# Norms passed in two halves of the tokens, with the output projection and the MLP in one block

## What is computed

```python
h = rmsnorm(x, norm_mix_pre)
q, k, v, gate, u = split(h @ w_in)            # mixer 1: retention, and an S5 scan over u with a GLU
mix = concatenate([y_ret, y_ssm]) @ w_out
x = x + rmsnorm(mix, norm_mix_post)
h = rmsnorm(x, norm_mlp_pre)
m = square(relu(h @ w_ff1)) @ w_ff2           # 1024 -> 4096 -> 1024
x = x + rmsnorm(m, norm_mlp_post)
hx = rmsnorm(x, pre_mix_g) * (1 + sc1) + sh1  # block 2: mixer with a two-way scan and a pool mixer
mix_x = mixer(hx)                             # ends in a projection by w_out_2
x = x + g1 * rmsnorm(mix_x, post_mix_g)
hm = rmsnorm(x, pre_mlp_g) * (1 + sc2) + sh2
x = x + g2 * rmsnorm(square(relu(hm @ w_mlp1_2)) @ w_mlp2_2, post_mlp_g)
```

## Time and profile before

| | us |
|---|---|
| median of 3 runs (lowest, highest) | 3440.88 (3438.74, 3441.52) |
| the profiled execution's own time | 3440.63 |
| its span, first to last instruction | 3438.8 |
| PE matmuls busy | 2934.4 (85%) |
| DVE busy | 1477.4 (43%) |
| POOL busy | 794.1 (23%) |
| ACT busy | 564.4 (16%) |

### The profile page before, as it was taken

The page is one execution under the profiler, slowest core; times in us unless marked ns, Lnnn a source line. Parts: engine busy times, 40 slices in busy tenths (PEclk is TensorE's granted clock), DMA queues, the critical chain, the costliest instruction groups (busy, mean ns, idle before and its releaser), DMA issues. The chain is left out here.

```text
span 3438.8 us, 35085 instructions
## 1 busy us (share of the span) xinstructions
PE 2934.4 (85%) x13838; PEld 2435.9 (71%) x13838; DVE 1477.4 (43%) x1676; ACT 564.4 (16%) x672; POOL 794.1 (23%) x417
## 2 busy tenths in 40 slices
PE   3987976978999999996987988847488799999996
PEld 3766765777888888875775767646367688888885
DVE  6365362243222222235655578856734422222224
ACT  3212213121110000012221112111111100000001
POOL 1110111212333333330211211102122233333331
PEclk9977988979999999995998998868787899999998
DMA  3121113101222122121000321231120111111111
GB/s 113 49 62 45 47 58 131 42 25 62 67 70 64 61 68 67 61 67 70 30 26 31 110 74 55 73 117 67 61 80 25 31 44 48 49 49 43 49 49 55
DMA packets 60736, 205.61 MB, mean 60 GB/s; under 512 B 10160, under 2 KB 13488, under 8 KB 60400
## 3 DMA queue, kind: packets, MB, share of 16 engines
q1 hardware_dynamic: 39072, 140.16, 12.4%
q10 hardware_dynamic: 21584, 64.40, 5.5%
HBM read 173.99 MB, written 29.36 MB: 59 GB/s over the span
## 5 line engine op out<-in xcount | busy, mean ns | idle before, releaser
L185 POOL CAST w_hi<-w_raw 128x1024 fp32r<-128x1024 f32 x206 | 221.6, 1076 | 2571.3 <-PE ps L198 2536.3
L194 PE MATMUL ps<-a_hi,w_hi 128*128 128x512 f32 x2176 | 707.8, 402 | 94.1 <-PEq L2170 21.6
L196 PE MATMUL ps<-a_lo,w_hi 128*128 128x512 f32 x2176 | 693.6, 395 | 0.0
L198 PE MATMUL ps<-a_hi,w_lo 128*128 128x512 f32 x2176 | 692.1, 394 | 0.0
L187 POOL TENSOR_TENSOR w_lo<-w_raw,w_hi 128x1024 fp32r<-128x1024 f32 x206 | 572.3, 2778 | 16.5
L194 PEld LDWEIGHTS ps<-a_hi,w_hi 128*128 128x128 f32 x2176 | 414.2, 193 | 182.2 <-issue 100.3
L196 PEld LDWEIGHTS ps<-a_lo,w_hi 128*128 128x128 f32 x2176 | 416.8, 192 | 88.9
L198 PEld LDWEIGHTS ps<-a_hi,w_lo 128*128 128x128 f32 x2176 | 415.5, 191 | 88.8
L194 PE MATMUL ps<-g_hi_b,w_hi 128*128 128x512 f32 x1120 | 352.2, 396 | 92.6 <-DVE g_lo_b L2121 56.1
L198 PE MATMUL ps<-g_hi_b,w_lo 128*128 128x512 f32 x1120 | 349.2, 393 | 0.0
L196 PE MATMUL ps<-g_lo_b,w_hi 128*128 128x512 f32 x1120 | 349.1, 393 | 0.0
(11 more groups left out here) (379 smaller groups left out, 2675.1 us busy)
## 6 DMA issues: line engine op xcount, KB each, us to landing
w_raw<-in_wstream SPq DMA_DIRECT2D x206, 512.0 KB, 3.5
ada_w<-in_ada_w ACTq DMA_DIRECT2D x50, 512.0 KB, 3.5
y_by_token<-y ACTq DMA_DIRECT2D x16, 512.0 KB, 2.7
tmp_b<-mixer_out SPq DMA_DIRECT2D x8, 512.0 KB, 3.3
x_res_b<-in_xT SPq DMA_DIRECT2D x1, 4096.0 KB, 13.8
x_block<-x_res_b SPq DMA_DIRECT2D x8, 512.0 KB, 2.6
u_rows<-ada_w ACTq DMA_DIRECT2D x8, 512.0 KB, 2.7
z_rows<-ada_w ACTq DMA_DIRECT2D x8, 512.0 KB, 2.7
```

The lines of the kernel that those rows point to most:

```text
L185: pool.tensor_copy(k.w_hi[:, s, :], k.w_raw[:, s, :]).then_inc(k.w_high, 1)
L194: pe.matmul(o, w_hi, a_hi[:, c], start=first, stop=False)
L196: pe.matmul(o, w_hi, a_lo[:, c], start=False, stop=False)
L198: ins = pe.matmul(o, w_lo, a_hi[:, c], start=False, stop=last)
```

## The change

Each norm is passed in two halves of 512 tokens. The output projection runs its 8 tiles for the first half, then for the second half; beside the second half, the first is normed. The MLP's first step is done in two half steps, and beside the first of them the second half is normed. The MLP's last step is done in two half steps too, and beside the second one the first half of the norm that follows is done. The norm's steps are now methods of a class `Turn`, each for one half, and are written into the other work's instructions at fixed places on each engine. The weights of the projection, the first and the last MLP step are used twice and stand twice in the stream (254 tiles in place of 206). Projection and MLP share one block. In the second layer, the part that needs the last hidden tile is moved behind both output tiles' other parts (`FIRST_ORDER`). The sum is no longer cleared: the first half steps copy in place of adding.

At the start, x tiles go to four buffers in place of two, the first two weight tiles are loaded between them, the high part is made by ACT straight from x with the gain as its scale and the low part by one DVE operation, the first GEMM runs as the tiles come, ahead of the norm's root, and the silu stands before the tiles. The loop over pairs of heads is written out on PE.

The core of the diff:

```diff
+NEXT_ORDER = [(half, kt) for half in range(2) for kt in range(HID)]
+FIRST_ORDER = [(half, kt) for half in range(2) for kt in range(HID - 1)] + [(half, HID - 1) for half in range(2)]
...
-P2_TILES = GLU_TILES + KT
-MLP_TILES = MLP_STEPS * 2 * HID
+P2_TILES = GLU_TILES + 2 * KT
+STEP_TILES = 2 * HID
+MLP_TILES = (MLP_STEPS + 2) * STEP_TILES
 XBC_END = P1_TILES + P2_TILES + MLP_TILES + XBC_TILES
 UZ_END = XBC_END + 2 * KT
-OUT2_END = UZ_END + 2 + 2 * KT
+OUT2_END = UZ_END + 2 + 3 * KT
 ALL_TILES = OUT2_END + MLP_TILES
 
...
+            def first_products(a, b):
+                for kt in range(a, b):
+                    pe.wait_ge(h_split, kt + 1)
+                    ins = tile_products(pe, k, 0, h_hi, h_lo, both_halves(k, 0), kts=1, at=kt * P, kt0=kt,
+                                        opens=kt == 0, closes=kt == KT - 1)
+                return ins
+            pe.wait_ge(k.w_split, 1)
+            first_products(0, KT - 2)
+            pe.wait_ge(x_sum, KT - 1)
             pe.wait_ge(ones_set, 2)
-            pe.wait_ge(const_in, 80)
             for c in range(NC):
-                ins = pe.matmul(Xf[0][:, c:c + 1], yc[:, c * P:(c + 1) * P], k.mean_col[:, :], start=True, stop=True)
+                ins = pe.matmul(Xf[0][:, c:c + 1], yc[:, c * P:(c + 1) * P], k.mean_col[:, :],
+                                start=c == 0, stop=False, skip_group_check=True)
+            pe.wait_ge(x_sq, KT)
+            for c in range(NC):
+                ins = pe.matmul(Xf[0][:, c:c + 1], qT[:, c * P:(c + 1) * P], k.mean_col[:, :],
+                                start=False, stop=True, skip_group_check=True)
             ins.then_inc(sums_done, 1)
+            first_products(KT - 2, KT).then_inc(k.tile_done, 1)
+            pe.wait_ge(const_in, 32)
             pe.wait_ge(inv_done, 1)
             for c in range(NC):
                 ins = pe.matmul(Xf[1][:, c * P:(c + 1) * P], rcol[:, c:c + 1].broadcast_to([P, P]), ident,
                                 start=True, stop=True)
             ins.then_inc(rstd_row, 1)
-            pe.wait_ge(h_split, KT)
             pe.wait_ge(silu_done, 1)
...
+    def sums_new_pe(self, pe, h, ts):
+        k, w = self.k, self.w
+        for t in ts:
+            pe.wait_ge(self.sq_new, h * KT + t + 1)
+            for c in range(HC):
+                at = (h * HC + c) * P
+                ins = pe.matmul(k.ps[:, 4 + h, c:c + 1], w.mix[:, t, at:at + P], k.mean_col[:, :],
+                                start=t == 0 and c == 0, stop=t == KT - 1, skip_group_check=True)
+        if KT - 1 in ts:
+            ins.then_inc(self.summed, 1)
...
+    def residual_dve(self, dve, ts, h):
+        k, w, cols = self.k, self.w, half_of(h)
+        dve.wait_ge(self.row, h + 1)
+        for t in ts:
+            dve.scalar_tensor_tensor(out=w.mix[:, t, cols], in0=w.mix[:, t, cols], scalar=self.gain(t),
+                                     in1=k.ps[:, 6 + h, :], op0=ALU.mult, op1=ALU.mult).then_inc(self.scaled, 1)
+            dve.wait_ge(self.scaled, h * KT + t + 1)
+            dve.tensor_tensor(w.x[:, t, cols], w.x[:, t, cols], w.mix[:, t, cols], ALU.add).then_inc(self.x_new, 1)
...
+    def split_dve(self, dve, ts, h):
+        k, w, cols = self.k, self.w, half_of(h)
+        dve.wait_ge(self.row_new, h + 1)
+        for t in ts:
+            if t >= 2:
+                dve.wait_ge(self.lo, h * KT + t - 1)
+            dve.scalar_tensor_tensor(out=w.tmp[:, t % 2, cols], in0=w.x[:, t, cols], scalar=self.following[0](t),
+                                     in1=k.ps[:, 6 + h, :], op0=ALU.mult, op1=ALU.mult).then_inc(self.raw, 1)
+            if t:
+                self.low_dve(dve, t - 1, h)
+        if KT - 1 in ts:
+            self.low_dve(dve, KT - 1, h)
...
+def output_halves_pe(pe, k, w, turn, n0):
+    for h in range(2):
+        for m in range(KT):
+            n, q = n0 + h * KT + m, m % 2
+            outs = [(k.ps[:, 2 * q + h, :], half_of(h))]
+            pe.wait_ge(k.w_split, n + 1)
+            pe.wait_ge(k.pair_free[q], n // 2)
+            tile_products(pe, k, q, w.a_hi, w.a_lo, outs, kts=KT // 2, closes=False)
+            if h and m == 1:
+                turn.row_pe(pe, 0)
+            if h and m == 3:
+                turn.sums_new_pe(pe, 0, range(KT // 2))
+            if h and m == 4:
+                turn.sums_new_pe(pe, 0, range(KT // 2, KT))
+            tile_products(pe, k, q, w.a_hi, w.a_lo, outs, kts=KT // 2, at=KT // 2 * P, kt0=KT // 2, opens=False)\
+                .then_inc(k.tile_done, 1)
+            if h and m == 0:
+                turn.sums_pe(pe, 0)
+            if h and m == 4:
+                turn.row_new_pe(pe, 0)
...
+def output_halves_dve(dve, turn, take):
+    for m in range(KT):
+        take(m, 0)
+        if m:
+            turn.add_dve(dve, m - 1, 0)
+    turn.add_dve(dve, KT - 1, 0)
+    take(0, 1)
+    turn.inverse_dve(dve, 0)
+    turn.add_dve(dve, 0, 1)
+    turn.residual_dve(dve, range(0, 2), 0)
+    take(1, 1)
+    turn.residual_dve(dve, range(2, 4), 0)
+    turn.add_dve(dve, 1, 1)
+    turn.residual_dve(dve, range(4, 6), 0)
+    take(2, 1)
+    turn.residual_dve(dve, range(6, KT), 0)
+    turn.add_dve(dve, 2, 1)
+    take(3, 1)
+    turn.add_dve(dve, 3, 1)
+    turn.inverse_new_dve(dve, 0)
+    take(4, 1)
+    turn.split_dve(dve, range(0, 1), 0)
+    turn.add_dve(dve, 4, 1)
+    turn.split_dve(dve, range(1, 4), 0)
+    take(5, 1)
+    turn.split_dve(dve, range(4, 5), 0)
+    turn.add_dve(dve, 5, 1)
+    turn.split_dve(dve, range(5, 7), 0)
+    take(6, 1)
+    turn.split_dve(dve, range(7, KT), 0)
+    turn.add_dve(dve, 6, 1)
+    take(7, 1)
+    turn.add_dve(dve, 7, 1)
...
+        def second_layer(t, q, banks, ready):
+            for half, kt in FIRST_ORDER if t == 0 else NEXT_ORDER:
+                if t == 0 and (half == 0 or kt == HID - 1):
+                    pe.wait_ge(s["hlo"], ready + kt + 1)
+                c = slice((half * HID + kt) * P, (half * HID + kt + 1) * P)
+                ins = products(pe, k.w_hi[:, q, c], k.w_lo[:, q, c], w.g_hi[:, kt, :], w.g_lo[:, kt, :],
+                               banks[half], kt == 0, kt == HID - 1)
+            return ins
+        def half_step(first, h, other):
+            n0, x0, g0 = tile_base(first, h), aux_uses(first, h), hidden_uses(first, h)
+            cols = half_of(h)
+            for t in range(HID):
+                n, q = n0 + t, t % 2
+                outs = [(k.ps[:, 2 * q + h, :], cols)]
+                pe.wait_ge(k.w_split, n + 1)
+                pe.wait_ge(k.pair_free[q], n // 2)
+                for kt in range(KT):
+                    if first and t == 0:
+                        pe.wait_ge(before.lo, h * KT + kt + 1)
+                    ins = tile_products(pe, k, q, w.a_hi, w.a_lo, outs, kts=1, at=kt * P, kt0=kt, opens=kt == 0,
+                                        closes=kt == KT - 1)
+                    if other and t == 1 and kt == KT // 2 - 1:
+                        other.row_pe(pe, 1 - h)
+                    if other and other.following and t == 3 and kt == KT // 2 - 1:
+                        other.sums_new_pe(pe, 1 - h, range(KT // 2))
+                ins.then_inc(k.tile_done, 1)
+                if other and t == 0:
+                    other.sums_pe(pe, 1 - h)
+                if A and h == 0:
+                    pe.wait_ge(s["ada_in"], (ada_index(first) + t + 1) * 16)
+                    pe.wait_ge(xs[q], x0 + t // 2)
+                    ada_products(pe, k, X[q][:, 0, :]).then_inc(ada_done, 1)
+            for t in range(HID):
+                n, q = n0 + HID + t, t % 2
+                pe.wait_ge(k.w_split, n + 1)
+                pe.wait_ge(k.pair_free[q], n // 2)
+                pe.wait_ge(xs[q], x0 + (A if h == 0 else 0) + t // 2)
+                second_layer(t, q, ([(k.ps[:, 2 * q + h, :], cols)], [(X[q][:, h, :], cols)]), g0)\
+                    .then_inc(k.tile_done, 1)
+                if other and other.following and t == 0:
+                    other.sums_new_pe(pe, 1 - h, range(KT // 2, KT))
+                if other and other.following and t == 1:
+                    other.row_new_pe(pe, 1 - h)
+        half_step(True, 0, before)
+        half_step(True, 1, None)
...
+        half_step(False, 0, None)
+        half_step(False, 1, turn)
+        turn.sums_pe(pe, 1)
+        turn.row_pe(pe, 1)
+        if turn.following:
+            turn.sums_new_pe(pe, 1, range(KT))
+            turn.row_new_pe(pe, 1)
...
+            square(0)
+            if other:
+                other.inverse_dve(dve, o)
+            low(0)
+            if other:
+                other.residual_dve(dve, range(0, 2), o)
+            square(1)
+            if other:
+                other.residual_dve(dve, range(2, 3), o)
+            low(1)
+            if other:
+                other.residual_dve(dve, range(3, 4), o)
+            square(2)
+            if other:
+                other.residual_dve(dve, range(4, 5), o)
+            low(2)
+            if other:
```

(108 more changed lines are left out.)

1210 lines of the change are left out of this document (640 added, 570 removed).

## The result

The changed kernel takes 3320.93 us (median of 4 runs, 3318.72 to 3323.84) where the kernel before takes 3441.2 (3438.74 to 3441.52): a ratio of 0.9651, 95% interval 0.9638 to 0.9663. The forecast was 3321. Its profiled execution has a span of 3318.5 us, 120.3 less than before, so the trace can be read stage by stage against the sum.

The account below looks back on a forecast made before the run. GEMMs were taken as bound by PE, the rest by chains of small steps between them. Gains of 38.7 + 37.0 + 10.3 + 12.8 + 12.6 + 8 = 119.4 us took 3440.6 to 3321, range 3280 to 3372.

Parts of the forecast that it names:

- bound 0 for one bank in a row: GEMM half tiles: 24 matmuls in a row into one PSUM bank cost nothing extra; other bound 0.12 us per matmul.
- First projection and MLP: First output projection to first MLP: both halves normed beside GEMMs, gain 38.7 us; 26.6 for the stretch after 12.1 inline.
- Lateness of DVE: Beside projection and MLP: DVE operations held by POOL make PE wait, costing 7 us in the first layer, 10.5 in the second.
- rival (1): Inline new sums beside GEMMs: the PE clock falls at ten blocks, costing 39 us, giving 3360; chance 0.14.
- Gap to the scan stage: First MLP to scan stage: only the first half hidden, tail 51.4 us in place of 73.8; gain 10.3 after inline work.
- Second projection and MLP: Second output projection to second MLP: norm hidden beside GEMMs, gain 37.0 us; 46.8 for the stretch with order and inline work.
- End: Second MLP to kernel end: tail 22.5 us, 15.6 less than before; net gain 12.8 after inline work.
- Order of the second layer: Second MLP: PE's eight waits for the last hidden tile go, gain 12.6 us, bounds 12.6 and 9.
- Start: Before the first projection: L650 at 39 to 44 us in place of 52.04; gain 8 us, bounds 13 and 3.
- Weight splits: POOL's splits beside half tiles: nothing paid; without cover, every us over 5.46 costs half a us on 96 half tiles.
- rival (4): Half tiles outrun POOL's weight split: slower than before if splits average 8.0 us; 3455 at 8.7; chance 0.04.
- the prediction's sign: Weight splits on POOL: all under 5.3 us would show the forecast right.

Follow-up runs that it names:

- the experiment: The parameter chain moved ahead of DVE's wait for the root's row, ACT's and DVE's head loops written out, against the changed kernel: 3309.8 us, 0.9627.

## Why the prediction was right, and where it was not

*The frame held.* What bounded the kernel, that the norms' chains would disappear beside GEMMs, and that their PE work would come back: 890.3 and 834.5 us against 890.5 and 831.3 by the sum. The half tile costs what a full one does by the column: 206 matmuls of 512 columns fill 626.8 to 673.5 us, 0.227 each, so bound 0 for one bank in a row was right.

That the sum came out within 0.1 us of the measured time is luck: it rests on errors that cancel.

*First projection and MLP*: the total is right by two errors against each other. The inline work was taken at 12.1 us a half; blocks of 3.49, 0.8 for the sums and 0.8 for each spread with 0.1 an interruption come to 9.9, so 6.6 us less in three halves. Lateness of DVE is 2 us, not 7. In their place stands what the sum left to rival (1): 9 us of matmuls at half clock. The step that failed is the choice of no clock loss in "a 1.84 us block between two tiles left the clock at 1.00": a block twice that long is not nearer to it than to the earlier trace rows. Of the rival's price the slow passes were wrong (three blocks of ten, not all) and the matmuls behind them right where they occur (1.6 to 2.5 against 2): 16 us, not 39.

*Lateness of DVE* was laid out with every operation on two SBUF tensors held until POOL's piece ends. The lock is there: these adds start just after POOL's operation and end just after it, 2.86 us where an undisturbed one takes 0.68. The Trainium skill ("SBUF — State Buffer", section "SBUF: two separate sides") says that the first holder blocks the other for its whole instruction; by that rule the trace agrees.

```profile
642.28 2.39 POOL L192 TENSOR_TENSOR w_lo<-w_raw,w_hi 128x1024 fp32r<-128x1024 f32 x1
...
642.36 2.86 DVE L951 TENSOR_TENSOR acc_b<-acc_b,tmp_b 128x512 f32<-128x512 f32 x1 [2.58 <-ACT tmp_b L915]
```

But the seven such adds beside the first half have 2.6 us or more of idle time before them, so holding them costs nothing, and of eight residual additions in the first projection five take 0.69 to 0.89. The term was mis-sized by holding all of them.

*Gap to the scan stage*: first sums 12.5 us after PE's end (14.3 forecast), gap 48.9 (51.4). Right, and the reordered list shows that 7.5 us of this wait were the order of DVE's list, not its work.

*Second projection and MLP*: 3.2 us under its term, with matmuls at half clock (6.3 us) in place of lateness again. *End*: 20.2 against 22.5.

*Order of the second layer*: the eight waits of 1.6 are gone. The half steps still wait 0.45 each and once 3.2.

*Start*: 4.6 against 8, the largest relative miss. The operation that was to start at 44 started at 49.92. The sum passes ended 5.3 us behind the last split and not 2 (6.4 us of them, most at half clock); the products of the last two input tiles, ahead of the row, took 4.9 us and not 2.8, at half clock; and the three row operations took 4.3 and not 3.7. The chain itself was left behind the row, as the sum had it and as the experiment shows it need not be.

*Weight splits*: "every us over 5.46 would cost half a us" is wrong. It treats the two slots as if each had its own POOL. Both are split in series, so the excess counts whole: with the 129 us that the two stretches lost at 1.75 us over, rival (4) decides at about 5.46 + 120 x 1.75 / 129 = 7.1 us a split, not 8.0. Nor does its "At 8.7 us it would give 3455" follow from its own rule, which gives 3321 + 96 x 1.62 = 3476. The longest split in the changed kernel is 5.90 us (2.29 + 3.52 at 1642, in the scan stage), over the 5.3 of the prediction's sign, but beside half tiles none is over 4.54, so the forecast did not suffer.

## What to carry to other kernels

When work moves beside a GEMM, price it by how it is cut: the same 64 small passes cost little more than their own length in eight pieces, half as much again in two blocks (19 us in five halves of 7.25), and nearly double in one (another 13, waits left out). On an engine with a fixed list, put first what another engine waits for, and let what is only needed later fill the waits of the new chain; that gained 7 us at the tail and 10 at the start without removing an operation. Then look again at who waits: with shorter passes PE ran into a wait for a square, and the cold matmuls behind it took back the gain of that stretch. And check a sum that comes out right stage by stage: here errors of 5 to 9 us stood against each other.

## What was not expected of the hardware

- A block of 32 one-column passes runs at full speed (3.49 us) and the 512-column matmuls behind it at half clock, 0.42 us apart for 3.4 to 5.3 us; that didn't happen behind three of ten such blocks, and not behind the same three in every kernel. Behind pieces of 0.95 us it happened once, where a modulation product followed (2.7 us of narrow matmuls in a row).
- Half clock can also follow short waits. Behind four waits of 2.45 us in the kernel with the old order matmuls are cold for 3 to 4 us; behind waits of 1.2 and 1.4 (at 793 and 2635 in the changed kernel) and one of 3.2 (at 3277) they aren't, and behind one of 1.8 with token sums after it (at 2576) they are.
- A DVE reciprocal of 512 columns takes 3.37 us, an addition of the same size 0.68 us.
- A small matmul of two columns on rounded data costs 0.12 us, one of one column in full precision two passes of 0.11.
- The untouched scan stage varies by 3 us between two executions of the changed kernel (901.9, 905.2) and from 900.2 to 906.4 over the kernels with the changed kernel's weight split: more than several terms of the sum.
